# Last block of a two-block transformer on one Trainium2 core: the token scale is taken out of the feed-forward input, and the last down projection and final norm are laid out with tokens on partitions

## The reference, cut to what matters

```
h  = h + merged @ w_out
u2 = rmsnorm(h, ffn_norm_w)                # h * rsqrt(mean(h^2)+eps) * w
a, val = split(u2 @ w_up, 2)               # 2816 + 2816 features
a  = causal_dwconv(a, ffn_conv_w, ffn_conv_b)   # three taps over tokens
h  = h + (silu(a) * val) @ w_down
return rmsnorm(h, final_norm_w)[:, N_META:]
```

## Time and profile before

| | before |
|---|---|
| median of 3 executions | 1200.36 us (1199.11 to 1201.03) |
| time of the profiled execution | 1200.52 us |
| its span | 1198.7 us |
| mean granted TensorE clock | 0.991 |
| HBM, mean over the span | 199 GB/s |

### The profile page before, as it was taken

One profiled execution on the slowest core, in us unless ns is written; L12 is line 12 of the kernel. 1 busy time (PEld: TensorE's weight loads), 2 busy tenths in 40 slices (PEclk: granted clock), 3 DMA queues, 4 the chain that ended last, 5 costly groups with the idle time before them and its releaser, 6 DMA issues.

```text
span 1198.7 us, 22749 instructions
## 1 busy us (share of the span) xinstructions
PE 1149.8 (96%) x8630; PEld 1088.2 (91%) x8630; DVE 878.9 (73%) x1486; ACT 616.6 (51%) x989; POOL 70.6 (6%) x134
## 2 busy tenths in 40 slices
PE   4999989999999999899999999999999999999997
PEld 4898679999888898799998889999999999999997
DVE  5799788998887985696554577787764766777643
ACT  4547546444336566654443465544443646555532
POOL 0101110211111310000000000000000000000000
PEclk9899989999999999999999999999999999999999
DMA  9947656999874743476455334433333453555531
GB/s 365 413 167 264 237 202 221 367 394 356 291 300 141 248 157 120 155 281 219 175 179 206 141 121 148 156 139 107 141 141 106 164 187 111 207 180 192 188 141 36
DMA packets 43131, 241.67 MB, mean 202 GB/s; under 512 B 5152, under 2 KB 7584, under 8 KB 20400
## 3 DMA queue, kind: packets, MB, share of 16 engines
q1 hardware_dynamic: 28912, 191.29, 44.3%
q0 software_dynamic: 14144, 49.37, 11.6%
HBM read 237.48 MB, written 1.06 MB: 199 GB/s over the span
## 4 chain that ended last, share of the span: by engine, by line
PE 82%; DVE 8%; ACT 5%; issue 3%; DMA 1%; SPq 0%; POOL 0%; DVEq 0%; ACTq 0%; POOLq 0%
PE acc L1914 20%; PE acc L1915 19%; PE acc L1916 19%; PE aux L2024 3%; PE aux L2026 3%; PE aux L2025 3%; PE aux L2401 2%; DVE wlo L1043 2%; ACT whi L583 1%; DMA x<-xT 1%; PE aux L1916 1%; PE aux L1914 1%; PE aux L1915 1%; ACT free_hlo L628 1%; PE aux L2055 1%
## 5 line engine op out<-in xcount | busy, mean ns | idle before, releaser
L1914 PE MATMUL acc<-hhi,whi 128*128 128x256 f32 (+3 forms) x1976 | 567.2, 287 | 6.8 <-DVE hlo L1064 4.0
L1915 PE MATMUL acc<-hlo,whi 128*128 128x256 f32 (+3 forms) x1976 | 560.2, 283 | 0.0
L1916 PE MATMUL acc<-hhi,wlo 128*128 128x256 f32 (+3 forms) x1976 | 557.7, 282 | 0.0
L1043 DVE TENSOR_TENSOR wlo<-raw,whi 128x1024 fp32r<-128x1024 f32 x338 | 412.8, 1223 | 178.6 <-ACT whi L583 178.1
L583 ACT ACTIVATE whi<-raw 128x1024 fp32r<-128x1024 f32 x338 | 357.1, 1057 | 189.7 <-PE acc L1916 119.4
L1914 PEld LDWEIGHTS acc<-hhi,whi 128*128 128x128 f32 x1976 | 374.0, 189 | 12.0 <-DVE hlo L1064 6.2
L1916 PEld LDWEIGHTS acc<-hhi,wlo 128*128 128x128 f32 x1976 | 375.7, 190 | 0.0
L1915 PEld LDWEIGHTS acc<-hlo,whi 128*128 128x128 f32 x1976 | 374.5, 190 | 0.2
L1072 DVE CUSTOM_DVE_ANT_0 lev<-lev,vec 128x1024 f32<-128x1024 f32 x56 | 71.7, 1280 | 1.9 <-DMA lev<-side_weights 1.9
L2026 PE MATMUL aux<-wlo,ahi 128*128 128x512 f32 x176 | 69.5, 395 | 0.0
L2024 PE MATMUL aux<-whi,ahi 128*128 128x512 f32 x176 | 69.4, 394 | 0.0
(11 more groups left out here) (372 smaller groups left out, 1518.0 us busy)
## 6 DMA issues: line engine op xcount, KB each, us to landing
raw<-weights SPq DMA_DIRECT2D x171, 1024.0 KB, 4.8
lev<-side_weights POOLq DMA_DIRECT2D x76, 512.0 KB, 6.0
qkv<-weights SPq DMA_DIRECT2D x3, 1024.0 KB, 14.6
x<-ln_rows POOLq DMA_DIRECT2D x6, 512.0 KB, 6.6
lev<-weights SPq DMA_DIRECT2D x2, 1024.0 KB, 20.1
big<-side_weights POOLq DMA_DIRECT2D x4, 512.0 KB, 5.7
big<-qkv POOLq DMA_DIRECT2D x32, 64.0 KB, 2.5
x<-gate_rows POOLq DMA_DIRECT2D x3, 512.0 KB, 6.9
```

The costliest lines, as they stand in the source:

```text
L1043: v.tensor_tensor(wlo[:, m % SPLIT, :], raw_unit(i, m), whi[:, m % SPLIT, :].bitcast(F32), ALU.subtract).then_inc(lo_ready, 1)
L1914: mm(o, whi[:, u % SPLIT, w], hi, start=start, stop=False, skip_group_check=True)
L1915: mm(o, whi[:, u % SPLIT, w], lo, start=False, stop=False, skip_group_check=True)
L1916: return mm(o, wlo[:, u % SPLIT, w], hi, start=False, stop=stop_, skip_group_check=True)
```

## The change

1. The feed-forward input of the last block no longer carries the token's scale: `hhi`/`hlo` are made of x times the norm's weight alone, tile by tile during `out2`. The squares are summed on VectorE and averaged by one matmul inside the first units of `ffn2` (plus two of one column that give the scale with tokens on partitions). The scale is applied to the a-results when VectorE moves them to `padded` (in place of ScalarE's copy), and at the very end to the down projection's result.
2. `down2` becomes kind rows. The residual is turned by 16 transposes between units 5, 7, 9 and 11 of `ffn2` and moved by four ScalarE copies.
3. The final norm works on four pieces of 128 tokens x 512 features: VectorE adds and multiplies by the final weight, ScalarE squares with a running sum, then Ln, Exp, and a last multiplication by VectorE (ScalarE for piece 2). The final weight is loaded as a row by one more GpSimd DMA of 512 KB behind the recurrence.

```
-    ("down2", 22, "deep"),
+    ("down2", 22, "rows"),
...
 scalar:
-            segment("out2", lambda i, j: None)
-            norm(5, T3, RMS_EPS, aux[1])
-            copy_hi(5, T3)
+            nc.scalar.preload_act_table_set("natural_log_exp_and_others")
+            def unscaled_high(j):
+                acc_read(act, None, START["out2"][2] + j)
+                A(hhi[:, j, 0:T3], x[:, j, T2 - T3:T2], ACT.Copy, scale=V("ffn_w", j)).then_inc(hhi_ready, 1)
+                A(big[:, 0, j * T3:j * T3 + T3], x[:, j, T2 - T3:T2], ACT.Square).then_inc(sq_ready, 1)
+            segment("out2", lambda i, j: unscaled_high(j - 1) if j else None, head=8)
+            unscaled_high(KT - 1)
+            def token_scales():
+                act.wait_ge(var_ready, 2)
+                st(A(std[:, 0:T3], aux[0][:, 0:T3], ACT.Ln, bias=RMS_EPS))
+                st(A(token_log, aux[0][:, 264:266], ACT.Ln, bias=RMS_EPS))
+                st.wait()
+                A(rstd[:, 0:T3], std[:, 0:T3], ACT.Exp, scale=-0.5)
+                A(token_rstd, token_log, ACT.Exp, scale=-0.5).then_inc(std_ready, 1)
...
 scalar, ffn2_unit:
+                if i is None and j == 0:
+                    token_scales()
+                if i is None and j in (6, 8, 10, 12):
+                    n = (j - 6) // 2
+                    act.wait_ge(x_turned, n + 1)
+                    A(tokens[:, 512 * n:512 * n + 512], aux[n][:, :], ACT.Copy).then_inc(x_moved, 1)
                 if j % 2 == 0:
-                    unit_done(act, i, m0f + j)
-                    A(padded[:, k % 2, 0:T3], acc[(a0f + j) % 4][:, 0:T3], ACT.Copy)\
-                        .then_inc(acc_free[(a0f + j) % 4], 1)
...
 scalar, end:
-            norm(6, T1, RMS_EPS, aux[1])
+            for b in range(4):
+                tok, half = divmod(b, 2)
+                act.wait_ge(z_summed, b + 1)
+                st(A(scratch[:, 512 * half:512 * half + 512], tokens[:, 512 * b:512 * b + 512], ACT.Square, accum_out=half_squares[b]))
+                st.wait()
+                if half == 0:
+                    st(A(half_bias[tok], half_squares[b], ACT.Identity, scale=1.0 / D, bias=RMS_EPS))
+                    st.wait()
+                else:
+                    st(A(final_log[tok], half_squares[b], ACT.Ln, scale=1.0 / D, bias=half_bias[tok]))
+                    st.wait()
+                    A(final_scale[tok], final_log[tok], ACT.Exp, scale=-0.5).then_inc(final_std, 1)
+            act.wait_ge(final_std, 2)
+            act.wait_ge(out_first, 3)
+            A(final_rows(2), final_rows(2), ACT.Copy, scale=final_scale[1]).then_inc(out_scaled, 1)
...
 vector, out2 and ffn2:
+            def residual(i, j):
+                unit_done(dve, i, m0o + j)
+                v.tensor_tensor(x[:, j, T2 - T3:T2], acc[(a0o + j) % 4][:, 0:T3], x[:, j, T2 - T3:T2], ALU.add)\
+                    .then_inc(acc_free[(a0o + j) % 4], 1)
+                if j:
+                    unscaled_low(j - 1)
+                    add_square(j - 1)
...
+                    if i is None and j == 0:
+                        dve.wait_ge(std_ready, 2)
+                    unit_done(dve, i, m0f + j)
+                    v.tensor_tensor(padded[:, k % 2, 0:T3], acc[(a0f + j) % 4][:, 0:T3], rstd[:, 0:T3], ALU.mult)\
+                        .then_inc(acc_free[(a0f + j) % 4], 1)
...
 vector, end:
+            def final_sum(b):
+                tok, half = divmod(b, 2)
+                if b < 3:
+                    dve.wait_ge(y_ready, 3 * 4 + b + 1)
+                else:
+                    unit_done(dve, None, SPLIT_UNITS - 1)
+                z = tokens[:, 512 * b:512 * b + 512]
+                v.scalar_tensor_tensor(z, row_banks[4][b][:, :], token_rstd[:, tok:tok + 1], z, ALU.mult, ALU.add).then_inc(z_summed, 1)
+                dve.wait_ge(z_summed, b + 1)
+                v.tensor_tensor(final_rows(b), z, final_gain[:, 512 * half:512 * half + 512], ALU.mult).then_inc(out_first, 1)
+            def final_part(b):
+                dve.wait_ge(final_std, b // 2 + 1)
+                dve.wait_ge(out_first, b + 1)
+                v.tensor_scalar(final_rows(b), final_rows(b), final_scale[b // 2], None, ALU.mult).then_inc(out_ready, 1)
...
+            for b in range(3):
+                final_sum(b)
+            final_part(0)
+            final_part(1)
+            final_sum(3)
+            final_part(3)
...
 tensor:
-            stats(5, T3, aux[1])
-            wide("ffn2", lambda j: (T3 - T1, T3) if j % 2 else (0, T3), h_ready, 40, first=3)
-            deep("down2", 2, T1)
-            stats(6, T1, aux[1])
+            def token_squares():
+                total = big[:, 0, 0:T3]
+                pe.wait_ge(squares_summed, KT - 1)
+                mm(aux[0][:, 0:T3], C("mean"), total, start=True, stop=True)
+                for tok in range(2):
+                    t = T3 - T1 + P * tok
+                    ins = mm(aux[0][:, 264 + tok:265 + tok], total[:, t:t + P], C("mean", 1), start=True, stop=True)
+                ins.then_inc(var_ready, 1)
+            def turn_residual(n):
...
+            wide("ffn2", lambda j: (T3 - T1, T3) if j % 2 else (0, T3), h_ready, 40, first=3, ahead=residual_pieces, head=12,
+                 between=lambda k: token_squares() if k == KT - 2 else None)
+            pe.wait_ge(x_moved, 4)
+            across(4, ahi, alo, lambda j: pe.wait_ge(a_ready, 2 * FT + j + 1), lambda j: j, depth=ROW_DEPTH[4])
```

More of the change, by code:

```diff
@@ L470, in build @@
         SEG = {name: n for name, n, _ in SEGMENTS}
-        ROW_SEGMENTS = ["out0", "down0", "out1", "down1"]
-        ROW_DEPTH = [1, 3, 1, 3]
+        ROW_SEGMENTS = ["out0", "down0", "out1", "down1", "down2"]
+        ROW_DEPTH = [1, 3, 1, 3, 3]
         def held(seg, j, on_scalar):
@@ L1441, in _ @@
             segment("even", lambda i, j: even_then(j), head=20, first=even_first)
-            def residual_wide(seg):
-                _, m0, a0 = START[seg]
-                def unit(i, j):
-                    unit_done(dve, i, m0 + j)
-                    v.tensor_tensor(x[:, j, T2 - T3:T2], acc[(a0 + j) % 4][:, 0:T3], x[:, j, T2 - T3:T2], ALU.add)\
-                        .then_inc(acc_free[(a0 + j) % 4], 1)
-                segment(seg, unit, head=8)
-            def residual_deep(seg):
-                segment(seg, nothing)
-                last = START[seg][1] + SEG[seg] - 1
-                for n in range(KT):
-                    if n < KT - 1:
-                        dve.wait_ge(y_ready, 3 * len(ROW_SEGMENTS) + n + 1)
-                    else:
-                        unit_done(dve, None, last)
-                    v.tensor_tensor(x[:, n, META:T2], deep_banks[n][:, 0:T1], x[:, n, META:T2], ALU.add).then_inc(y_read, 1)
             def ffn_tiles(seg, f, between):
@@ L1860, in _, with unscaled_low, add_square @@
             merged_low(7)
-            residual_wide("out2")
-            rms(5, 5, "ffn_w", T3)
+            _, m0o, a0o = START["out2"]
+            def unscaled_low(k):
+                dve.wait_ge(hhi_ready, 40 + k + 1)
+                v.scalar_tensor_tensor(hlo[:, k, 0:T3], x[:, k, T2 - T3:T2], V("ffn_w", k), hhi[:, k, 0:T3].bitcast(F32),
+                                       ALU.mult, ALU.subtract).then_inc(h_ready, 1)
+            def add_square(k):
+                if k:
+                    total = big[:, 0, 0:T3]
+                    dve.wait_ge(sq_ready, 4 + k + 1)
+                    if k > 1:
+                        dve.wait_ge(squares_summed, k - 1)
+                    v.tensor_tensor(total, total, big[:, 0, T3 * k:T3 * k + T3], ALU.add).then_inc(squares_summed, 1)
+            def residual(i, j):
[5 more added lines that the diff above has]
+                    add_square(j - 1)
+            segment("out2", residual, head=8)
+            unscaled_low(KT - 1)
+            add_square(KT - 1)
             _, m0f, a0f = START["ffn2"]
@@ L1899, in _ @@
                 low2(None, k)
[L1900 to L1904 removed]
+            segment("down2", nothing)
+            def final_sum(b):
+                tok, half = divmod(b, 2)
+                if b < 3:
+                    dve.wait_ge(y_ready, 3 * 4 + b + 1)
+                else:
+                    unit_done(dve, None, SPLIT_UNITS - 1)
[7 more added lines that the diff above has]
+                v.tensor_scalar(final_rows(b), final_rows(b), final_scale[b // 2], None, ALU.mult).then_inc(out_ready, 1)
+            dve.wait_ge(final_loaded, 16)
+            dve.wait_ge(x_moved, 4)
+            for b in range(3):
[4 more added lines that the diff above has]
+            final_part(3)
         @block.tensor
@@ L1922, in needed, with wide @@
                 return T2 - T3, T2
-            def wide(seg, span, ready=None, before=0, tiles=1, ahead=None, head=1, of=(hhi, hlo), tail=0, first=0, turned=None, late=0):
+            def wide(seg, span, ready=None, before=0, tiles=1, ahead=None, head=1, of=(hhi, hlo), tail=0, first=0, turned=None, late=0, between=None):
```

(18 more changed lines are left out.)

80 lines of the change are left out of this document (42 added, 38 removed).

## The result

The changed kernel takes 1188.97 us (median of three executions, 1188.96 to 1191.07) where the kernel before takes 1200.36: ratio 0.9913, interval 0.989 to 0.9935 (all ratios here are of means; here 1189.67 to 1200.17). The forecast was 1192.3 with a range from 1190.0. The profiled execution took 1188.96 us, its span is 1187.2.

The account below looks back on a forecast made before the run. TensorE, busy 1149.8 of 1198.7 us, was taken as the bound except where it stands still. Terms -5.8 + 0.8 + 0 + 2.0 - 1.05 - 4.0 = -8.05 us gave 1192.3 us, range 1190.0 to 1196.0.

Parts of the forecast that it names:

- The gap: Between out2 and ffn2: TensorE's 6.8 us without useful work goes, about 1.0 us is inserted; net -5.8 us.
- The averages: Inserted in ffn2's first units: one fp32 matmul of 258 columns and two of one column, 1.0 us in all.
- the change of kind: At the inserted averages: 0.1 us allowed for TensorE's switch to another kind of matmul.
- The stall ahead of unit 4: Early ffn2: TensorE waits for unit 4's split, behind VectorE's wait for the scale and the convolution; +0.8 us.
- The scaling on VectorE: Rest of ffn2: the scaling replaces ScalarE's copy and fits in VectorE's idle time; zero.
- The price behind the cover: In ffn2, about 0.5 us idle a pair is the cover; each 0.1 us beyond costs at most 2.2 us.
- the rival that VectorE becomes the bound: In ffn2, VectorE's work in a pair exceeds TensorE's 5.75 us, so the kernel gets slower; chance 0.04.
- The transposes: In ffn2, sixteen transposes at full price in TensorE's list, 0.45 to 0.5 us for four; +2.0 us.
- Down2: As rows it takes down1's 61.43 us where it took 62.48; -1.05 us.
- The tail: Behind down2's last product: 6.3 us to the span's end where it was 10.3; -4.0 us.
- The clock: Rival: one-column matmuls or transposes lower TensorE's clock in ffn2, 3.5 to 5 us lost, 1196 to 1197; chance 0.06.
- the last line of the sum: Whole kernel: the -8.05 us taken from the profiled 1200.52 gives 1192.5, and the median 0.16 us below gives 1192.3.

Follow-up runs that it names:

- split_first: Changed kernel with VectorE's split of ffn2's fifth weight unit ahead of the first convolution's last two instructions; 197.01 us from last out2 product to end.
- one_more: Changed kernel with one more VectorE instruction in each pair of ffn2's units, behind the convolution; ratio 0.9922.
- two_more: Changed kernel with two more VectorE instructions in each pair of ffn2's units, behind the convolution; ratio 0.9918.
- the doubled ones: Changed kernel with each of the sixteen transposes of the residual issued twice, in the same four groups and banks; ratio 0.9925.
- hhi_alone: Kernel before with unused tiles placed so that hhi and hlo alone start at a multiple of 64 bytes; ratio 0.9999.
- before_pad64: Kernel before with an unused 64-byte tile behind vec, so hhi still starts 32 bytes above a multiple of 64; ratio 1.0002.
- before_pad32: Kernel before with an unused 32-byte tile behind vec, so hhi starts at a multiple of 64 bytes; ratio 0.9994.

## Why the prediction was wrong, step by step

- **The gap** (forecast -5.8): -6.07, from the last product of out2 to the last of ffn2's unit 3 (the mean over both profiles of each kernel). The averages took 0.80 us, not 1.0, of which the two of one column are 0.37 (997.88 to 998.25) and not 0.46. The forecast's 0.1 us for the change of kind rested on no row; behind the averages one product starts 0.08 us later than a spacing (998.25 to 998.45). Right.
- **The stall ahead of unit 4** (forecast +0.8): the place and the cause were right, shown by split_first, which removes it, and by one_more and two_more, which lengthen it. The size was 0.38 (0.27 ahead of the unit, 0.1 inside it). ScalarE's chain ended 1.17 us after the averages (998.25 to 999.42, the end of the row below), not 1.4, and the averages were shorter. The forecast's own terms also add up to 1005.77, not 1005.85 (1002.6 + 0.43 + 0.15 + 1.37 + 1.22).

```profile
999.23 0.19 ACT L1015 ACTIVATE std<-std 128x2 f32<-128x2 f32 x1
```

- **The scaling on VectorE** (forecast 0): 0. The price behind the cover, 2.2 us for each 0.1 us a pair, was an upper bound far too high: the splits' lead of 4.6 us stands behind the idle time. So the rival that VectorE becomes the bound stood further off than I made it.
- **The transposes** (forecast +2.0): +1.76, by the doubled ones +1.74. A group costs 0.44 us. The earlier trace rows gave just that (441.56 - 441.00 - 0.12), and four times 1.76; I rounded it up to 0.45 to 0.5 and to 2.0.
- **Down2** (forecast -1.05): -1.04. **The tail** (forecast 6.3 us, -4.0): 6.30. Bank 3 was taken 0.30 us behind the slot, not 0.65 (the two scalings ahead of it take 0.88 us, not 1.1); from the end of ScalarE's last copy (1184.05) to the end it took 3.1 us, not 2.9, and the steps between took 2.87, not 2.75 (bank 3's sum to that copy's end), so that three small errors cancel. That the total fits is luck in part.
- **What no term had**: from unit 5 of ffn2 on, the stretch to down2 grew by 0.23 us beyond the transposes. The placing of the tiles alone moves this stretch by as much: from the last out2 product to the end, hhi_alone takes 206.46 us and before_pad64 206.40, where before takes 206.19. The two differ in where hhi stands within 64 bytes, so it is not that start alone; the cause is open.
- Together -8.8 where the sum was -8.05: 0.76 us of the miss is in the terms, in the stall (0.4), the averages (0.3) and the transposes (0.24), less that last 0.23.
- **The clock** (a rival, 0.06): it did not fall in ffn2. One reading behind that rival was wrong: amid the one-column matmuls the clock was still 1.00, and 0.51 only behind them.

```profile
22.00:26.00 4.00, 4.00 (x37) 1.00 1.01 422
```


The step that failed is the last line of the sum: "The profiled execution took 1200.52, so 1192.5 us; the median is 0.16 us below it". It takes one execution's level for the kernel's and the time ahead of out2 as the same in both. With the terms as measured it would have given 1191.5 us (1200.36 - 8.81), inside the range; what lies below that is this step. The level: 78 executions of the kernel before, over all the runs, have a median of 1199.29 us (1197.1 to 1201.5), so 1.1 us of the miss lies in the starting point. The part ahead: the diff's line on `vec` moved hhi and hlo to multiples of 64 bytes, which in the two profiles compared gives about -1.2 us (-0.55 of it in ffn1, most of the rest in ffn0, small ones of both signs behind), and in the mean of executions perhaps -0.6, which is not clear of noise. The rest of the profiles' 2.75 us is mostly which stretches ran at half clock: the changed kernel's profile had the shorter one at the first and the second place (-1.2 and -0.8) and the longer one at the third (+0.7); 0.25 us is left over. Of the miss of 3.3 us that leaves 0.9 (3.3 - 0.76 - 1.1 - 0.6), which no run assigns. The median rests on three executions, and those of one kernel differ by more: ten or more of them spread over 2.3 to 5.3 us. At the first two places both families have both values, so that is chance as far as the runs show. The third is not: its longest form stands only where hhi starts at a multiple of 64 bytes.

What stays open is why the start of hhi changes the third place, and how much of the products' 1.2 us that takes back. The stretch of 28.8 us belongs to that start (seven profiles of ten, none of the other six), and its cost over 28.0 goes the right way; the means are too wide to put a figure on it.

## What to carry to other kernels

A sum against one profiled execution carries that execution's luck: read the granted clock at each pause of TensorE ahead of the change, and put the spread of executions into the range, even where every term is certain. A line that only shortens a small tile moves all tiles behind it, and the rate of fp32 products can hang on where their moving operand starts (0.5% here). A gain in one part can be taken back by the clock in another, so compare the spread of executions too, and not only their middle. An engine's idle time is not all of its cover: look also at how far ahead of its use each of its results is finished.

## What the runs showed that I had not expected

- Products of 256 fp32 columns (fp32r) come in 2.853 us for 24 when the moving operand starts 32 bytes above a multiple of 64 bytes, and in 2.840 us at a multiple, at the same granted clock and with TensorE busy throughout. Sixteen profiles, no exception. In ffn2, where every second unit starts two columns in, there was no gain.
- Eight transposes of 128x128 fp32 in a stream of products take 0.80 us start to start, and the granted clock stays at 1.00.
- One kernel's executions spread over up to 5 us of 1200 (before_pad32: 1196.4 to 1201.2). Its five with a mean granted clock of 0.989 average 1200.7 us and its five with 0.993 or more 1196.9. The time from out2 to the end agreed to 0.03 us in two profiles each of two kernels.
- Where a tile starts also goes with how long TensorE runs at half clock: a mean granted clock of 0.989 or less in 25 of 59 executions with hhi at a multiple of 64 bytes, and in none of 100 with hhi 32 bytes above one.
